# A mixed-attention decoder step on one core: three reorderings in its first stage (a copy, an activation, a projection piece)

## The reference, cut to what matters

```python
def even_layer(x, ...):
    h = rmsnorm(x, norm_g)
    q, kvc, kvs, kvw, gt, z, xbc, dtr = split_cols(h @ w_in, EVEN_SPLITS)
    o_nsa = nsa_mixer(q, sigmoid(gt), kv_cmp, kv_slc, kv_win, ...)
    o_ssm, ssm_new, conv_new = mamba_mixer(z, xbc, dtr, conv0, ssm0, ...)
    x = x + concatenate([o_nsa, o_ssm]) @ w_out

def compress_blocks(rows, pe, w1, w2):      # in nsa_mixer, for keys and for values
    h = einsum('bnlgd,ldh->bngh', rows + pe, w1)
    return einsum('bngh,hd->bngd', gelu(h), w2)

def mamba_mixer(...):
    acc = conv_b + sum(xpad[:, k:k + L] * conv_w[k] for k in range(4))
    xs, bm, cm = split_cols(silu(acc), ...)
    y, s_final = ssd_scan(xs, dt, a, bm, cm, ssm0)     # chunks of 128 tokens
```

## Time and profile before

| what | us |
|---|---|
| three timed runs | 3090.65, 3074.84, 3086.92 (median 3086.92) |
| the profiled execution, its device time | 3074.78 |
| its span on the core | 3073.0 |
| what lies around the span | 1.8 |
| TensorE busy in the span | 2963.0 (96%) |
| VectorE busy | 1031.5 (34%) |
| ScalarE busy | 628.7 (20%) |
| mean granted TensorE clock | 0.979 of full speed |

### The profile page before, as it was taken

One profiled execution on the slowest core, in us unless ns is written; L12 is line 12 of the kernel. 1 busy time (PEld: TensorE's weight loads), 2 busy tenths in 40 slices (PEclk: granted clock), 3 DMA queues, 4 the chain that ended last, 5 costly groups with the idle time before them and its releaser, 6 DMA issues.

```text
span 3073.0 us, 44117 instructions
## 1 busy us (share of the span) xinstructions
PE 2963.0 (96%) x18651; PEld 2688.2 (87%) x18651; DVE 1031.5 (34%) x2193; ACT 628.7 (20%) x1215; POOL 663.5 (22%) x354
## 2 busy tenths in 40 slices
PE   6999999999988999999999999988999999999998
PEld 5866756667767999999999999877999999999998
DVE  2102124676655332222212242266242222122224
ACT  3002121266643210010000022144120000000014
POOL 1020100011112322223222322102322223222320
PEclk9999998999998999999999999988999999999999
DMA  4625221021063111111111111100111111111111
GB/s 146 213 71 144 93 82 28 32 72 29 2 183 100 42 42 42 42 55 42 42 42 55 42 42 49 48 1 15 28 42 42 44 53 42 42 42 55 42 55 59
DMA packets 209478, 179.69 MB, mean 58 GB/s; under 512 B 36730, under 2 KB 190383, under 8 KB 208690
## 3 DMA queue, kind: packets, MB, share of 16 engines
q1 hardware_dynamic: 202272, 148.79, 16.3%
q0 software_dynamic: 6848, 28.04, 3.1%
q10 hardware_dynamic: 162, 0.04, 0.0%
HBM read 162.44 MB, written 19.51 MB: 59 GB/s over the span
## 4 chain that ended last, share of the span: by engine, by line
PE 90%; DVE 4%; SPq 2%; issue 2%; ACT 1%; DMA 0%; DVEq 0%; ACTq 0%
PE ps L2092 51%; PE ps L594 8%; PE ps L719 4%; PE ps L2108 4%; PE ps L2126 3%; PE ps L590 3%; PE ps L1390 2%; PE ps L2504 2%; PE ps L1403 2%; PE ps L1426 2%; PE ps L2728 1%; SPq L1716 1%; PE ps L2488 1%; PE ps L2367 1%; PE ps L1049 1%
## 5 line engine op out<-in xcount | busy, mean ns | idle before, releaser
L2092 PE MATMUL ps<-spot,w_hi 128*128 128x368 f32 (+1 forms) x6156 | 1185.3, 327 | 1.5 <-DVE arena L2217 0.8
L2092 PEld LDWEIGHTS ps<-spot,w_hi 128*128 128x128 f32 x6156 | 1035.4, 188 | 2.3 <-DVE arena L2217 1.4
L2092 PE MATMUL ps<-spot,w_lo 128*128 128x368 f32 (+1 forms) x3132 | 686.0, 327 | 0.0
L2092 PEld LDWEIGHTS ps<-spot,w_lo 128*128 128x128 f32 x3132 | 537.3, 188 | 0.0
L2068 POOL CAST w_hi<-arena 128x2048 fp32r<-128x2048 f32 x79 | 154.6, 1957 | 1374.1 <-DMA arena<-in_w_gate_up 761.5
L2069 POOL TENSOR_TENSOR w_lo<-arena,w_hi 128x2048 fp32r<-128x2048 f32 x78 | 363.2, 4656 | 6.3
L2217 DVE TENSOR_TENSOR arena<-arena,ps 128x368 f32<-128x368 f32 (+1 forms) x312 | 147.1, 527 | 428.3 <-PE ps L2092 354.6
L594 PE MATMUL ps<-arena 128*128 128x368 f32 (+1 forms) x768 | 245.1, 477 | 1.5 <-DVE arena L1218 1.5
L594 PEld LDWEIGHTS ps<-arena 128*128 128x128 f32 x768 | 147.0, 194 | 88.1 <-issue 6.3
L2308 ACT ACTIVATE arena<-arena 128x1088 f32<-128x1088 f32 x44 | 49.0, 1113 | 831.4 <-DVEq L2324 831.4
L2328 DVE TENSOR_TENSOR arena<-arena,ps 128x368 f32<-128x368 f32 x132 | 62.3, 527 | 443.5 <-PE ps L2092 438.3
(11 more groups left out here) (450 smaller groups left out, 3160.9 us busy)
## 6 DMA issues: line engine op xcount, KB each, us to landing
arena<-in_w_gate_up SPq DMA_DIRECT2D x88, 512.0 KB, 4.7
arena<-in_w_down SPq DMA_DIRECT2D x22, 1024.0 KB, 4.9
arena<-in_cache_nsa_cmp_kv SPq DMA_DIRECT2D x128, 128.0 KB, 2.2
arena<-in_cache_nsa_slc_kv SPq DMA_DIRECT2D x128, 128.0 KB, 2.6
arena<-in_w_in_even SPq DMA_DIRECT2D x9, 1024.0 KB, 6.3
x_spill<-arena POOLq DMA_DIRECT2D x1, 4352.0 KB, 14.7
arena<-in_x_prompt SPq DMA_DIRECT2D x8, 512.0 KB, 6.5
arena<-in_cmp_w_k POOLq DMA_DIRECT2D x16, 256.0 KB, 4.5
```

Source lines behind the costliest of these rows:

```text
L2092: mm = nc.tensor.matmul(ps[:, 3 * s + j, 0:b - a], w, x[:, a:b], start=m == 0, stop=m == len(order) - 1)
```

## The change

Three edits, all in the order of instructions; no product, activation or transfer is added or taken away.

1. In `front_act`, the root of the first tile stands ahead of the loop. In a step, ScalarE now copies the raw turn of that same step's tile, then forms the root of the next tile, and then evicts.
2. The Gelu of the second compression batch stands ahead of the last Silu, not behind it.
3. In the scan, one of the two pieces of chunk 0 stands between `before(0)` and `before(1)`; one stays behind.

```diff
             evict = Evict(act, True)
+
+            def root(i):
+                n = tile_n(i)
+                x_loaded(act, i)
+                E.chain(nc.scalar.activation(sq_junk[0:n], xin[i][0:n], ACT.Square, accum_out=rtok[0:n, i:i + 1]))
+                nc.scalar.activation(rtok[0:n, i:i + 1], rtok[0:n, i:i + 1], ACT.Sqrt, scale=1.0 / D_MODEL, bias=eps_c[0:n])\
+                    .then_inc(sem("rtok"), 1)
+
+            root(0)
             for step in range(NT + 2):
                 if step < NT:
                     i, n = step, tile_n(step)
-                    x_loaded(act, i)
-                    E.chain(nc.scalar.activation(sq_junk[0:n], xin[i][0:n], ACT.Square, accum_out=rtok[0:n, i:i + 1]))
-                    nc.scalar.activation(rtok[0:n, i:i + 1], rtok[0:n, i:i + 1], ACT.Sqrt, scale=1.0 / D_MODEL, bias=eps_c[0:n])\
-                        .then_inc(sem("rtok"), 1)
-                if 1 <= step <= NT:
-                    i, n = step - 1, tile_n(step - 1)
                     act.wait_ge(sem("raw_tr"), i + 1)
                     for h in range(2):
                         mm = nc.scalar.copy(xraw[:, 4 * h:4 * h + 4, toks(i)],
                                             ps[:, 2 + h, 0:4 * n].rearrange("p (c t) -> p c t", c=4))
                     mm.then_inc(sem("x_raw"), 1)
+                if step + 1 < NT:
+                    root(step + 1)
                 if step >= 2:
                     evict()
...
+            hidden_act(act, 1)
             silu_act(act, XC - 1)
-            hidden_act(act, 1)
             evict(2)
...
             for c in range(PT):
                 n, s = P, (c + 1) % 2
+                if c == 0:
+                    piece(1)
                 if c + 1 < PT:
                     before(c + 1)
                 if c == 1:
                     scores_pe(pe)
-                piece(SSM_PIECES[c])
+                piece(SSM_PIECES[c] - (c == 0))
```

## The result

| | us |
|---|---|
| the kernel before, median of 8 runs beside the changed one | 3076.05 (3064.96 to 3090.65) |
| the changed kernel, median of 8 runs | 3055.32 (3044.56 to 3064.72) |
| ratio, 95% interval | 0.9923 (0.9899 to 0.9946) |
| profiled span, before and after | 3073.0 and 3055.0 |

The forecast was 3052.8, within 3037 to 3073, and faster. The ratio means about 24 us; the medians differ by 20.7, the spans of the two profiles by 18.0. The forecast gain was 29.0, taken from 3081.8.

The account below looks back on a forecast made before the run. TensorE bounds the kernel (90% of the chain): its work, waits and the clock lost after them. Edits of 15.1, 7.5 and 6.4 us sum to 29.0, taken from the mean 3081.8: 3052.8 us, range 3037 to 3073.

Parts of the forecast that it names:

- edit 1: three waits for the copy: Front, odd steps: raw turns no longer wait for ScalarE's copy behind eviction and root; 3 x 2.97 = 8.9 us.
- edit 1: step 1: Front, step 1: tile 0's copy runs while rows are on their way, turn starts at about 14.7; 2.5 us.
- edit 1: clock: Front: the clock falls behind two of three waits go with the waits; 2 x 1.85 = 3.7 us.
- edit 2: wait: End of the convolution: TensorE's 4.99 us wait for the Gelu shrinks to 0.1; 4.9 us saved.
- edit 2: clock: The piece behind the Gelu wait takes 4.95 us at full clock, not 7.59; 2.6 us more.
- edit 3: First prompt chunks: wait ahead of `before(1)` and its slow clock go; 6.4 us (3.9 wait, 2.5 clock).
- first stage together: All three edits: 15.1 + 7.5 + 6.4 = 29.0 us; without any clock given back 20.2.
- the wait of step 7: Front, step 7: a like wait but no clock fall, the step taking 5.83 us where full clock takes 5.64.
- the input rows of later tiles: Front: behind 14.6 us no wait for input rows; later tiles there 2.5 to 11 us sooner is a choice.
- SP's pages: Ahead of the first compression product: page loads move with the last normed turn, 2.8 us margin, costed at nothing.
- the 2.66 us for a switch: Edit 2's table load: by this price edit 2 gives 1.4 us less; one chance in ten, inside the forecast.
- The fourth rival: Behind 600 us: the clock falls more often; at a mean of 0.96 it costs 51 us, 3104; 5%.

Follow-up runs that it names:

- the old order: ScalarE's order without edit 1: the kernel before (median 3076.05 us), and that kernel with only edit 2 (ratio 0.9989) or only edit 3 (0.9983).
- edit 2 alone: Only the second Gelu put ahead of the last Silu, against the kernel before; ratio 0.9989 (0.9967 to 1.0010).
- the root back: The changed kernel with each tile's root at the head of its own step again, ahead of the copy; 3058.92 us, run once.
- the eviction first: The changed kernel with the eviction at the head of ScalarE's step, ahead of the copy; 3059.29 us, run once.
- the split: The changed kernel with one piece moved ahead of the sample's operands, 3068.36 us; with second-batch page numbers also read ahead of SP's wait, 3049.99 us.
- the changed kernel, third profile: The changed kernel without further edit, run beside the one with both further edits; 3052.09 us, ratio 0.9928 (0.9906 to 0.9950).

## Why the prediction was right

**The sum.** Term by term, from marks that don't depend on where the stage begins:

| term | forecast | measured |
|---|---|---|
| edit 1: three waits for the copy | 8.9 | 8.9 (all gone) |
| edit 1: step 1 | 2.5 | 2.1 (first piece at 20.86, and 22.98 before) |
| edit 1: clock | 3.7 | 3.7 in this pair, 1.9 against the other two profiles of the old order (one fall each) |
| edit 2: wait | 4.9 | 4.84 (4.99 to 0.15) |
| edit 2: clock | 2.6 | 2.45, less 1.5 in the two pieces behind (11.37 against 9.88) |
| edit 3 | 6.4 | 6.6 |
| wait for the second batch's pages | 0 | -0.4, chance |
| the last turns ahead of attention | 0 | -0.8, chance |
| first stage together | 29.0 | 26.3 (the rows above give 25.9; the turns behind the wait of step 7 and L731 behind its own wait took 0.2 us each more before) |

**Edit 1.** Each step of the argument held: the copy behind the eviction was the wait, the input rows of later tiles were there in time, and SP's pages moved with the last normed turn (first product at 130.03 against 129.9). What was too sure was the clock. Old-order steps with a wait of 2.97 us are in three profiles, nine in all, and four of them had the 1.85 us: two in the first profile, one in each other. The expected price was about 2.5 us and not 3.7. The wait for the second batch's pages, which I did not cost, was 0.4 us longer in this pair. That is not the edit's doing: it is 0.8, 1.1 and 1.7 us in the three profiles with the old order, 0.7, 1.3 and 1.5 in the three of the changed kernel.

**Edit 2.** Right in its mechanism and in the wait to 0.1 us. The piece behind it takes 5.14 us at full clock, where I had read 4.95 off another one: 0.2 us. The gap between Silu, table load and Gelu is 0.02 us again, the load 1.28, and so the 2.66 us for a switch in the Trainium skill (ScalarE: Activation LUTs, What ACT_TABLE_LOAD costs) would have been wrong by 1.4 us for TensorE's wait here. What I missed is that a part of the clock can be lost again 10 us later: 11.4 us for two pieces in all three profiles of the changed kernel and with edit 2 alone, 9.9 where the slow piece stood ahead of them, as in the kernel before. But they took 9.9 too with the root back and with the eviction first, so this loss comes in some executions and not by the order alone.

**Edit 3.** Right: 6.6 us, with the clock. An operand block behind dense pieces takes 2.89 us (448.13 to 451.02 in the changed kernel), where I had 3.08.

**The total.** The medians differ by 20.7 us in the first comparison, by 26.2 and 24.2 in the next two (3082.36 to 3056.19, 3076.29 to 3052.09), which fits 26.3 in the first stage and chance in the rest. I put the sum on the mean of four executions, 3081.8, rather than on the median of three or the profile, a guess at a spread whose cause I did not know. The kernel before then had a median of 3076.05: my base was 5.8 us too high, and the gain of 29.0 was 8.3 above the 20.7 between the medians. The two errors cancel but for 2.5 us, so that 3055.32 lies this near to 3052.8 is luck; that the mechanisms held is not. A part of the spread has a name now. In the first pair of profiles, the changed kernel had the slow pace in the feed-forward of layer 1 and the other one had not (848.6 against 839.3), which took 9 of the 26 us out of the difference of the spans. The fourth rival, a loss behind 600 us, was thus real as chance, but by pace and not by the granted clock; it also shows that one pair of profiles can't price an edit under 10 us by its spans.

**What stays open.** Why the two pieces ahead of the sample's result had the slow clock in some kernels. With the order of the changed kernel there they took 11.3 to 11.4 us in four profiles (the changed kernel's three and edit 2 alone), 12.8 in one and 9.88 in two; in both kernels with the split they had full clock. The order alone is not the cause, and two of two against two of seven doesn't show that the split prevents it. In the first four of these profiles the clock had also fallen behind the second batch's wait (the chunk there took 6.2 us), in the two with 9.88 it had not (5.54), so what happens there may depend on what went before; no run tests it. And what chooses the pace in the feed-forward: it settles at the last wait of TensorE in the stage (0.3 to 0.4 us for VectorE) and stays to the stage's end, in kernels with either outcome.

## What to carry to other kernels

Where an engine serves a ring of buffers, put what frees a buffer ahead of what only drains an output: three waits of 3 us were one copy standing behind an eviction and a root, and both could come later. The additional table load here took ScalarE 1.28 us out of a wait of 3.7 us, and TensorE nothing; price such a reorder by what waits behind it, not by the number of loads. For edits under half a per cent read marks inside the stage, over several profiles, and compare the stages behind them one by one before charging a difference to the edit.

## What the runs showed of the hardware that I had not expected

**Two paces at one clock.** In the long dense stages a stretch of 40 us holds 245 or 242 passes (164.4 or 166.7 ns from start to start), at a granted clock of 1.00, with weight loads and products both busy all the time and no wait. Of twelve profiles, two had the slow pace in the dense stage of layer 0 (897 us instead of 887) and seven in that of layer 1 (848 instead of 839). The same program showed both. Each costs 9 to 10 us; as an estimate from this, the two together could make most of the spread of 20 us between runs of one kernel, but no timed run beside the profiled ones shows its pace.

**What stood behind TensorE's waits.** All at this kernel's places; a fall is a stretch at a granted clock of 0.50.

| wait of TensorE | falls | cost of one |
|---|---|---|
| 1.6 us, between dense products (eviction first) | 0 of 3 | |
| 2.97 us, at the same place (old order) | 4 of 9 | 1.85 us |
| 3.93 us, ahead of small turns | 3 of 3 | 1.6 to 2.5 us |
| 2.54 us, ahead of the last small turns of the stage | 12 of 12 | not worked out |
| 5.0 us, ahead of the keys' product | 3 of 3 | 1.8 to 2.5 us |
| 0.7 to 1.7 us, ahead of the second batch's first chunk | 7 of 10 | 0.9 us |

The length alone doesn't decide. In the last row of the table a wait of 0.67 us had a fall (the changed kernel, third profile: the chunk took 6.22 us) and one of 0.74 had none (the root back: 5.54, and 5.32 without a wait). Nor does a fall need a wait. In every profile the clock fell inside the 128 tiny products L1124, 2 to 6 us into them, with TensorE busy, and not only behind the wait of 1.48 us that follows. In the changed kernel (L1131 there) they run from 468.57 to 478.37, and from 472 to 476 the granted clock was 0.61 with TensorE busy in all of the 4 us.

The Trainium skill (TensorE: Matmul & The Clock Gate, The HAM clock gate) has the throttled clock as the default, released by activity. The falls behind the long waits agree with it; what decides between two like waits, the rows don't show.
